# A fused two-block layer stack on one core: 24 extra matmuls of one other form in each weight unit of the last stage

## The chip, the cores and the metric

The kernel runs on one core of a Trainium2 chip. The metric is the device time of one execution in microseconds (us), as the median over the runs shown. Engines: TensorE (PE in the profile, its weight loads PEld), VectorE (DVE), ScalarE (ACT), GpSimd (POOL), SyncE (SP, which issues most DMAs).

## What is computed

The activation has 256 tokens of 2048 features. Four layers run one after the other: two of a first kind (a pooling or a recurrent mixer, a gated output product, and a second gated product), two of a second kind. The second kind, which ends the program, is in short:

```python
def hybrid_layer(x, ...):
    h = rms_norm(x, norm_g)
    proj = h @ w_in
    ...
    y_a = mla_branch(...) * jax.nn.silu(z_a)
    y_b = sgu_branch(...) * jax.nn.silu(z_b)
    y_c = gla_branch(...) * jax.nn.silu(z_c)
    g = jax.nn.sigmoid(gate_logits...).reshape(B, S, N_BRANCH, D)
    merged = (g[:, :, 0] * (y_a @ w_branch[0])
              + g[:, :, 1] * (y_b @ w_branch[1])
              + g[:, :, 2] * (y_c @ w_branch[2]))
    return x + merged @ w_out
```

All data are fp32. The last stage of the program is `merged @ w_out` of the last layer, a 256x2048 by 2048x2048 product, and the sum with x.

## The kernel before

**Weights.** The weights of all layers lie in DRAM as one stream of 1144 units. A unit is eight tiles of 128x128 fp32 (512 KB). SyncE loads unit n into one of four slots of `raw`. ScalarE writes its copy rounded to `fp32r`, TensorE's reduced fp32, into `w_hi` (line 890), VectorE the rest raw - w_hi into `w_lo` (line 1272). The semaphores `raw_in`, `hi_done`, `lo_done` and `pe_mark` pass a unit from one engine to the next and free its slots.

**Activations.** They are kept feature by feature in partitions, a tile of 128 features at a time, with the rounded value of the 256 tokens in columns 0:256 and the rest in columns 256:512. `xs` (16 tiles) holds a stage's normed input, `inner`, `latent`, `y_abc` and `merged` the inner ones. A tile of `xs` is 512 fp32 long in a partition, so neighbouring tiles lie 2 KiB apart.

**A unit on TensorE.** In `products` (lines 515 to 548) a tile of weights is stationary and 256 columns stream. For each of the eight tiles of a unit, `w_hi` times the rounded value (line 535) and `w_hi` times the rest (line 536), 16 matmuls; then TensorE waits for `lo_done` and does `w_lo` times the rounded value (line 543), eight matmuls. The last of these frees the unit's slots.

```python
if c == 0:
    if side is not None:
        side.run(at_unit(s, i, u) - 1)
    pe.wait_ge(lo_done, unit)
```

A product of the last stage has 16 tiles deep, thus two units, and ends in a bank of PSUM that VectorE evicts (line 1713), adding x. Every tensor instruction is issued with its own weight load.

**Other streams.** Stages whose result is wanted token by token (`token_products`, lines 550 to 575) exchange the operands: 128 columns of `xs` are stationary, and 512 columns of `w_hi` (line 565) or `w_lo` (line 573) stream, eight and four of them a unit. Attention, gated linear attention and norms are plain fp32 matmuls, put between the high and the low matmuls of a unit (`side.run`) or around them: line 742 (one column), line 624 (128 columns, `keep_warm`), line 874 (256 columns), line 657 (64 columns, which `g_q` yields in blocks of 1, 2, 4 or 8 neighbours with gaps as wide as the block). Each is recorded as two matmuls.

**PSUM.** Eight banks: four in `banks`, one `ms_bank`, three in `pm`. The last stage uses `banks` alone.

**The last stage.** It is named `wo`, has four turns of four products, eight units a turn and 32 in all, and no side work. VectorE and ScalarE only split weights and evict in it. SyncE stores the results, the last four tiles one by one (line 497).

Of the kernel before, what the change touches and what calls it, by code (L numbers as in the profile page):

```python
# [21 lines left out]
P = 128  # L22
HALF = P // 2
T = 256
# [141 lines left out]
def build(nc, weights, x_in, p_in, channels, inv_counts, tables, positions, w_a2, w_s, b_s, x_scratch,  # L166
          out):
    with ExitStack() as ctx:
        def sb(name, shape, dt=F32, into=ctx):
            return into.enter_context(nc.sbuf_tensor(name, shape, dt))  # L170
# [6 lines left out]
        w_hi = sb("w_hi", [P, SLOTS, UNIT], F32R)  # L177
        w_lo = sb("w_lo", [P, SLOTS, UNIT], F32R)
        sb("xs_offset", [P, 112])
        xs = sb("xs", [P, ND, 2 * T], F32R)  # L180
# [25 lines left out]
        def place(name, at, shape, dt=F32):  # L206

            with ExitStack() as over:
                if at:
                    sb(f"under_{name}", [P, int(at * 256)], F32, over)  # L210
                return sb(name, shape, dt, over)[:]

        inner, wide = place("inner", 0, [P, NI, 2 * T], F32R), place("wide", 64, [P, NI, T])
# [5 lines left out]
        y_abc, merged = place("y_abc", 0, [P, 24, 2 * T], F32R), place("merged", 48, [P, ND, 2 * T], F32R)  # L219
# [32 lines left out]
        pm = ctx.enter_context(nc.psum_tensor("pm", [P, 3, 2 * T], F32))  # L252
# [48 lines left out]
        stages = []  # L301
# [80 lines left out]
        def at_unit(s, i, u):  # L382

            return s.unit0 + i * s.units + u - named[s.layer, "latent"].unit0
# [35 lines left out]
        def read_of(s, i, j):  # L420

            e = s.readers[j]
            return READ[e], i * s.readers.count(e) + (s.read0[e] + s.readers[:j + 1].count(e))
# [5 lines left out]
        def product_bank(s, i, j):  # L429

            b, half = s.bank(i, j), slice(T, 2 * T) if s.fed and i == 1 else slice(0, T)
            if s.by_token:
                half = slice(0, 2 * T)
            return banks[:, b, half] if b < BANKS else pm[:, b - BANKS, half]

        def occupant(s, i, j):

            n, b = stages.index(s), s.bank(i, j)
            while True:
                j -= 1  # L440
                if j < 0:
                    i, j = i - 1, s.width - 1
                if i < 0:
                    n -= 1
                    if n < 0:
                        return None
                    s = stages[n]
                    i, j = s.turns - 1, s.width - 1
                if s.bank(i, j) == b:
                    return s, i, j  # L450
# [63 lines left out]
        def _(pe):  # L514
            def products(s, i, ready, after, side):
                tile = 0
                for j, p in enumerate(s.products):
                    bank = product_bank(s, i, j)
                    held = occupant(s, i, j)
                    if held is not None:  # L520
                        pe.wait_ge(*read_of(*held))
                    k = 0
                    while k < p.depth:
                        u, c = divmod(p.first_tile + k, UNIT_TILES)
                        n = min(p.depth - k, UNIT_TILES - c)
                        slot = (s.unit0 + u) % SLOTS
                        unit = i * s.units + (s.unit0 + u + 1)
                        if c == 0:
                            pe.wait_ge(hi_done, unit)
                        for t in range(n):  # L530
                            if ready is not None:
                                ready(j, k + t)
                            w = slice((c + t) * P, (c + t + 1) * P)
                            x = p.operand(i, k + t)
                            nc.tensor.matmul(bank, w_hi[:, slot, w], x[:, 0:T], start=(k + t == 0), stop=False)  # L535
                            nc.tensor.matmul(bank, w_hi[:, slot, w], x[:, T:2 * T], start=False, stop=False)  # L536
                        if c == 0:
                            if side is not None:
                                side.run(at_unit(s, i, u) - 1)
                            pe.wait_ge(lo_done, unit)  # L540
                        for t in range(n):
                            w = slice((c + t) * P, (c + t + 1) * P)
                            ins = nc.tensor.matmul(bank, w_lo[:, slot, w], p.operand(i, k + t)[:, 0:T],  # L543
                                                   start=False, stop=(k + t == p.depth - 1))
                        ins.then_inc(pe_mark, 1)
                        k += n
                    if after is not None and j == after[0]:
                        after[1]()

            def token_products(s, i, side):  # L550

                for j in range(2):
                    held = occupant(s, i, j)
                    if held is not None:
                        pe.wait_ge(*read_of(*held))
                depth, per_unit = s.units * UNIT_TILES // 4, UNIT_TILES // 4
                for u in range(s.units):
                    slot, unit = (s.unit0 + i * s.units + u) % SLOTS, i * s.units + (s.unit0 + u + 1)
                    pe.wait_ge(hi_done, unit)
                    for r in range(per_unit):  # L560
                        k, w = u * per_unit + r, slice(r * 2 * T, (r + 1) * 2 * T)
                        x = s.products[0].operand(i, k)
                        for j in range(2):
                            for at in (j * P, T + j * P):
                                nc.tensor.matmul(product_bank(s, i, j), x[:, at:at + P], w_hi[:, slot, w],  # L565
                                                 start=(k == 0 and at < T), stop=False)
                    side.run(at_unit(s, i, u) - 1)
                    pe.wait_ge(lo_done, unit)
                    for r in range(per_unit):
                        k, w = u * per_unit + r, slice(r * 2 * T, (r + 1) * 2 * T)  # L570
                        x = s.products[0].operand(i, k)
                        for j in range(2):
                            ins = nc.tensor.matmul(product_bank(s, i, j), x[:, j * P:(j + 1) * P],  # L573
                                                   w_lo[:, slot, w], start=False, stop=(k == depth - 1))
                    ins.then_inc(pe_mark, 1)
# [249 lines left out]
            for n, s in enumerate(stages):  # L825
# [7 lines left out]
                elif s.name in ("squared", "wo"):  # L833
                    def ready(j, k, b=stages[n - 1].base["p"]):
                        if j == 0:
                            pe.wait_ge(pool_done, b + k + 1)
# [20 lines left out]
                for i in range(2 if s.fed else 1 if s.by_rows else 0, s.turns):  # L857
                    if s.by_token:
                        token_products(s, i, side)
                        continue  # L860
                    if s.name == "pooled":
                        pe.wait_ge(tile_split, i * 8 + 8)
                    elif s.name == "lru":
                        pe.wait_ge(pool_done, stages[n - 1].base["p"] + i * 8 + 8)
                    products(s, i, None if i else ready, after, side)
# [1385 lines left out]
```

## Time and profile before

| what | us |
|---|---|
| median of two runs | 3346.53 |
| the two runs | 3344.90 and 3348.15 |
| span of the profiled execution, first to last instruction | 3361.6 |
| TensorE busy in it | 3322.8 (99%) |
| VectorE busy | 2291.6 (68%) |
| ScalarE busy | 1670.6 (50%) |
| GpSimd busy | 905.0 (27%) |

The page gives of the profiled execution only its span, which is longer than both timed runs. A row of a group of instructions tells its line, engine, operation, what it writes and reads, its shape and how often it stands there, then busy time and the mean duration of one. A matmul's duration holds its way through the array, in which the next one already runs, so durations of neighbours overlap. In a timeline the first number is the start in us from the span's start, the second the time from the first start to the last end of the instructions merged into the row, and a number in brackets the engine's idle time ahead of it.

### The profile page before, as it was taken

The numbers are of one execution on the slowest core, as the hardware profiler recorded it, in microseconds if no ns is written. First come the engines' busy times: TensorE is split into PE (matmuls) and PEld (weight loads), VectorE is DVE, ScalarE is ACT, GpSimd is POOL, SyncE is SP. The second block draws the span as 40 slices with busy tenths as digits, with TensorE's granted clock in tenths as the row PEclk, the third lists the DMA queues.
The fourth block names the chain that finished last, engine by engine and source line by source line (L and its number), as shares of the span: only waits on it lengthen the run. The fifth ranks groups of instructions, "written<-read, shape, count | busy, mean of one in ns | idle before, by whom it ended". The sixth has DMA issues, their size and how long they took to land.

```text
span 3361.6 us, 65406 instructions
## 1 busy us (share of the span) xinstructions
PE 3322.8 (99%) x27748; PEld 3275.0 (97%) x27748; DVE 2291.6 (68%) x2982; ACT 1670.6 (50%) x2108; POOL 905.0 (27%) x839
## 2 busy tenths in 40 slices
PE   8999999999999999999999999999999999999999
PEld 8999999999999999999899999999999999999999
DVE  7876654588878854777877755555668787655554
ACT  5334444555578844655554544444455544444443
POOL 4952320053556610332423210000004232100000
PEclk9999999999999999999999999999999999999999
DMA  6555565555655575545454455555654544555655
GB/s 233 185 186 186 187 214 188 176 185 184 198 182 181 182 237 196 176 162 181 150 172 153 156 194 195 195 194 194 195 180 166 171 152 151 190 194 193 195 191 180
DMA packets 170050, 620.20 MB, mean 184 GB/s; under 512 B 18976, under 2 KB 20640, under 8 KB 169376
## 3 DMA queue, kind: packets, MB, share of 16 engines
q1 hardware_dynamic: 165888, 602.23, 54.1%
q10 hardware_dynamic: 3872, 13.80, 1.1%
q8 instruction: 219, 3.59, 0.4%
q14 instruction: 71, 0.58, 0.1%
HBM read 610.71 MB, written 4.19 MB: 183 GB/s over the span
## 4 chain that ended last, share of the span: by engine, by line
PE 85%; DVE 6%; ACT 4%; POOL 3%; issue 1%; DMA 0%; ACTq 0%; POOLq 0%; DVEq 0%; SPq 0%
PE banks L543 20%; PE banks L535 20%; PE banks L536 20%; PE banks L565 4%; PE pm L543 3%; PE pm L536 3%; PE pm L535 3%; DVE w_lo L1272 2%; POOL win L2005 2%; PE banks L573 2%; ACT w_hi L890 2%; PE banks L607 2%; PE banks L600 2%; PE banks L602 1%; PE pm L607 1%
## 5 line engine op out<-in xcount | busy, mean ns | idle before, releaser
L1272 DVE TENSOR_TENSOR w_lo<-raw,w_hi 128x1024 fp32r<-128x1024 f32 x1144 | 1475.5, 1294 | 878.7 <-ACT w_hi L890 863.7
L890 ACT ACTIVATE w_hi<-raw 128x1024 fp32r<-128x1024 f32 x1144 | 1204.7, 1057 | 1013.0 <-PE banks L543 645.8
L535 PE MATMUL banks<-xs,w_hi 128*128 128x256 f32 x4008 | 950.0, 279 | 0.3 <-ACT val L1156 0.2
L536 PE MATMUL banks<-xs,w_hi 128*128 128x256 f32 x4008 | 949.8, 279 | 0.0
L535 PEld LDWEIGHTS banks<-xs,w_hi 128*128 128x128 f32 x4008 | 757.8, 189 | 0.9 <-ACT val L1156 0.7
L536 PEld LDWEIGHTS banks<-xs,w_hi 128*128 128x128 f32 x4008 | 757.6, 189 | 0.2
L543 PE MATMUL banks<-xs,w_lo 128*128 128x256 f32 x4008 | 553.0, 280 | 1.2 <-DVE w_lo L1272 1.2
L543 PEld LDWEIGHTS banks<-xs,w_lo 128*128 128x128 f32 x4008 | 500.6, 189 | 2.0 <-DVE w_lo L1272 1.6
L1929 POOL CAST merged<-act 128x256 fp32r<-128x256 f32 x32 | 41.1, 1285 | 714.7 <-DVE act L1709 714.7
L535 PE MATMUL pm<-xs,w_hi 128*128 128x256 f32 x952 | 223.4, 277 | 0.0
L536 PE MATMUL pm<-xs,w_hi 128*128 128x256 f32 x952 | 223.1, 277 | 0.0
L535 PE MATMUL banks<-inner,w_hi 128*128 128x256 f32 x896 | 215.5, 279 | 0.0
L536 PE MATMUL banks<-inner,w_hi 128*128 128x256 f32 x896 | 215.3, 279 | 0.0
L535 PEld LDWEIGHTS pm<-xs,w_hi 128*128 128x128 f32 x952 | 178.9, 188 | 0.1
L536 PEld LDWEIGHTS pm<-xs,w_hi 128*128 128x128 f32 x952 | 178.9, 188 | 0.1
L535 PE MATMUL banks<-y_abc,w_hi 128*128 128x256 f32 x768 | 178.8, 276 | 0.0
L536 PE MATMUL banks<-y_abc,w_hi 128*128 128x256 f32 x768 | 178.8, 276 | 0.0
L536 PEld LDWEIGHTS banks<-inner,w_hi 128*128 128x128 f32 x896 | 169.1, 189 | 0.0
L535 PEld LDWEIGHTS banks<-inner,w_hi 128*128 128x128 f32 x896 | 169.0, 189 | 0.0
L535 PEld LDWEIGHTS banks<-y_abc,w_hi 128*128 128x128 f32 x768 | 144.2, 188 | 0.0
L536 PEld LDWEIGHTS banks<-y_abc,w_hi 128*128 128x128 f32 x768 | 144.1, 188 | 0.0
L1929 POOL CAST inner<-act 128x256 fp32r<-128x256 f32 x64 | 72.6, 1134 | 259.2 <-DVE act L1754 178.2
(335 smaller groups left out, 5956.8 us busy)
## 6 DMA issues: line engine op xcount, KB each, us to landing
raw<-weights SPq DMA_DIRECT2D x1144, 512.0 KB, 3.4
wide<-x_in ACTq DMA_DIRECT2D x4, 512.0 KB, 8.7
wide<-x_in ACTq DMA_DIRECT2D x1, 2048.0 KB, 11.7
x_scratch<-wide ACTq DMA_DIRECT2D x1, 2048.0 KB, 8.5
wide<-x_scratch ACTq DMA_DIRECT2D x1, 2048.0 KB, 10.9
out_x<-wide SPq DMA_DIRECT2D x3, 512.0 KB, 6.3
w_st<-w_s ACTq DMA_DIRECT2D x2, 512.0 KB, 4.4
b_st<-b_s ACTq DMA_DIRECT2D x2, 512.0 KB, 5.3
```

The costliest lines, as they stand in the source:

```text
L535: nc.tensor.matmul(bank, w_hi[:, slot, w], x[:, 0:T], start=(k + t == 0), stop=False)
L536: nc.tensor.matmul(bank, w_hi[:, slot, w], x[:, T:2 * T], start=False, stop=False)
L543: ins = nc.tensor.matmul(bank, w_lo[:, slot, w], p.operand(i, k + t)[:, 0:T], start=False, stop=(k + t == p.depth - 1))
L565: nc.tensor.matmul(product_bank(s, i, j), x[:, at:at + P], w_hi[:, slot, w], start=(k == 0 and at < T), stop=False)
L573: ins = nc.tensor.matmul(product_bank(s, i, j), x[:, j * P:(j + 1) * P], w_lo[:, slot, w], start=False, stop=(k == depth - 1))
L600: nc.tensor.matmul(bank, w_hi[:, slot, w], operand[:, k, 0:T], start=(k == 0 and j < 4), stop=False, skip_group_check=True)
L602: nc.tensor.matmul(bank, w_hi[:, slot, w], operand[:, k, T:2 * T], start=False, stop=False, skip_group_check=True)
L607: ins = nc.tensor.matmul(bank, w_lo[:, slot, w], operand[:, k, 0:T], start=False, stop=(k == s.products[0].depth - 1), skip_group_check=True)
L890: nc.scalar.activation(w_hi[:, slot, :], raw[:, slot, :], ACT.Copy).then_inc(hi_done, 1)
L1272: nc.vector.tensor_tensor(w_lo[:, slot, :], raw[:, slot, :], w_hi[:, slot, :].bitcast(F32), ALU.subtract).then_inc(lo_done, 1)
L1929: link(nc.gpsimd.tensor_copy(dest[:, 0:T], source))
L2005: link(nc.gpsimd.tensor_tensor(dst[:, PAD:], src[:, PAD:], src[:, back:back + T], ALU.add))
```

## The change

The function `products` calls a new one, `other_shapes`, once in each unit of the last stage, ahead of the wait for `lo_done`. It issues 24 matmuls into the three banks of `pm`, every one with `start` and `stop`, so nothing is summed, and nothing reads them. The form depends on the unit (n from 0 to 31): which columns of `xs` stream (start, order, number), which tile of `w_hi` is stationary, and for the last two units the operands are exchanged.

By width, the 32 units are: 256 columns in 17 (ten starts; four other orders; one with a fixed stationary tile; two with stationary tiles that begin 16 or 64 columns further), 512 columns in ten (four starts; three other orders; a fixed stationary tile; two exchanged), and one each of 192, 224, 128, 384 and 320 columns. Together that is 10,720 columns times 24. Four of the orders read two neighbours at a time: `[[0, P], [1, 2]]` and `[[0, T], [1, 2]]` the same two again and again, `[[2, 64], [512, 2], [1, 2]]` and `[[2, P], [512, 2], [1, 2]]` two of one tile and two of the next in turn.

```diff
--- before.py
+++ after.py
@@ -537,6 +537,8 @@
                         if c == 0:
                             if side is not None:
                                 side.run(at_unit(s, i, u) - 1)
+                            if s is stages[-1]:
+                                other_shapes(i * s.units + u, slot)
                             pe.wait_ge(lo_done, unit)
                         for t in range(n):
                             w = slice((c + t) * P, (c + t + 1) * P)
@@ -546,6 +548,42 @@
                         k += n
                     if after is not None and j == after[0]:
                         after[1]()
+
+            def other_shapes(n, slot):
+
+                def moving(source, at, dims):
+                    return bass.AP(tensor=source.tensor, offset=source.offset + at, ap=[list(source.ap[0])] + [list(d) for d in dims])
+
+                x, m, h = xs[:, 0, :], merged[:, 0, :], w_hi[:, slot, :]
+                line = lambda n_: [[1, n_]]
+                tile = lambda c, at=0: moving(h, at + (c % 7) * P, line(P))
+                wide = lambda b: pm[:, b % 3, :]
+                part = lambda n_: (lambda b: pm[:, b % 3, 0:n_])
+                row = lambda c, at=0: c % 4 * 512 + at
+                shapes = (
+                    [(part(T), tile, lambda c, a=a: moving(x, row(c, a), line(T)))
+                     for a in (0, 16, 32, 48, 64, 80, 96, 112, 8, 4)]
+                    + [(part(T), tile, lambda c: moving(x, row(c, P), [[-P, 2], [1, P]])),
+                       (part(T), tile, lambda c: moving(x, row(c), [[0, P], [1, 2]])),
+                       (part(T), tile, lambda c: moving(x, row(c), [[2, 64], [512, 2], [1, 2]])),
+                       (part(T), tile, lambda c: moving(x, row(c), [[32, 16], [1, 16]]))]
+                    + [(part(n_), tile, lambda c, n_=n_: moving(x, row(c), line(n_))) for n_ in (192, 224, 128)]
+                    + [(wide, tile, lambda c, a=a: moving(x, row(c, a), line(512))) for a in (0, 32, 64, 96)]
+                    + [(wide, tile, lambda c: moving(x, row(c), [[0, T], [1, 2]])),
+                       (wide, tile, lambda c: moving(x, row(c), [[512, 2], [1, T]])),
+                       (wide, tile, lambda c: moving(x, row(c), [[2, P], [512, 2], [1, 2]]))]
+                    + [(part(n_), tile, lambda c, n_=n_: moving(x, row(c), line(n_))) for n_ in (384, 320)]
+                    + [(part(T), lambda c: tile(0), lambda c: moving(x, row(c), line(T))),
+                       (wide, lambda c: tile(0), lambda c: moving(x, row(c), line(512))),
+                       (part(T), lambda c: tile(c, 16), lambda c: moving(x, row(c), line(T))),
+                       (part(T), lambda c: tile(c, 64), lambda c: moving(x, row(c), line(T))),
+                       (wide, lambda c: moving(x, c % 7 * P, line(P)), lambda c: moving(h, 16 + c % 2 * T, line(512))),
+                       (wide, lambda c: moving(x, c % 7 * P, line(P)), lambda c: moving(h, 64 + c % 2 * T, line(512)))]
+                )
+                if n < len(shapes):
+                    to, stationary, streamed = shapes[n]
+                    for c in range(24):
+                        nc.tensor.matmul(to(c), stationary(c), streamed(c), start=True, stop=True, skip_group_check=True)
 
             def token_products(s, i, side):
 
```

TensorE's instructions in two units of the last stage (`x24` or `x8` is that many alike in a row), before:

```order
L535 MATMUL banks<-merged,w_hi 128x256
L536 MATMUL banks<-merged,w_hi 128x256
L535 MATMUL banks<-merged,w_hi 128x256
L536 MATMUL banks<-merged,w_hi 128x256
L543 MATMUL banks<-merged,w_lo 128x256 x8
L535 MATMUL banks<-merged,w_hi 128x256
L536 MATMUL banks<-merged,w_hi 128x256
L535 MATMUL banks<-merged,w_hi 128x256
L536 MATMUL banks<-merged,w_hi 128x256
```

and in the changed kernel at the same place:

```order
L535 MATMUL banks<-merged,w_hi 128x256
L536 MATMUL banks<-merged,w_hi 128x256
L535 MATMUL banks<-merged,w_hi 128x256
L536 MATMUL banks<-merged,w_hi 128x256
L586 MATMUL pm<-xs,w_hi 128x256 x24
L545 MATMUL banks<-merged,w_lo 128x256 x8
L535 MATMUL banks<-merged,w_hi 128x256
L536 MATMUL banks<-merged,w_hi 128x256
L535 MATMUL banks<-merged,w_hi 128x256
```

Between the last high-weight matmul and the eight low-weight ones, whose line is now 545, stands a row of 24 on line 586.

Further on in TensorE's stream, around the narrow forms and the first wide one, units 14 to 17 of the stage, the rows of line 586 of the changed kernel, and ahead of each the last of the stage's own high-weight matmuls:

```order
L536 MATMUL banks<-merged,w_hi 128x256
L586 MATMUL pm<-xs,w_hi 128x192 x24
L545 MATMUL banks<-merged,w_lo 128x256 x8
L536 MATMUL banks<-merged,w_hi 128x256
L586 MATMUL pm<-xs,w_hi 128x224 x24
L545 MATMUL banks<-merged,w_lo 128x256 x8
L536 MATMUL banks<-merged,w_hi 128x256
L586 MATMUL pm<-xs,w_hi 128x128 x24
L545 MATMUL banks<-merged,w_lo 128x256 x8
L536 MATMUL banks<-merged,w_hi 128x256
L586 MATMUL pm<-xs,w_hi 128x512 x24
L545 MATMUL banks<-merged,w_lo 128x256 x8
```

Here the width of the burst goes from 192 to 224, 128 and 512 columns; the stage's own matmuls stay as they were.

## Rows read from the trace of the kernel before

**Rows 1.** The page's first part: busy us (share of the span) xinstructions.

```profile
PE 3322.8 (99%) x27748; PEld 3275.0 (97%) x27748; DVE 2291.6 (68%) x2982; ACT 1670.6 (50%) x2108; POOL 905.0 (27%) x839
```

**Rows 2.** Who waited for whom, 3273 us to the end: us in total, times, longest.

```profile
ACT w_hi L890 <- PE banks L543: 47.4, 29, 1.7
DVE w_lo L1272 <- ACT w_hi L890: 29.6, 27, 1.5
...
DVE wide L1713 <- PE banks L543: 12.8, 16, 5.0
```

**Rows 3.** TensorE in the last stage: stretch, us, busy (records), granted clock, DMA share, GB/s.

```profile
3273.40:3358.60 85.20, 85.20 (x754) 1.00 0.56 184
```

**Rows 4.** Line 543 in the last stage: duration ns, first and last start.

```profile
L543 PE MATMUL banks<-merged,w_lo x256: 276/276/276, 3273.5 to 3358.6; 128*128 128x256 f32 x128
```

**Rows 5.** TensorE's timeline in the first unit of the last stage: start, us.

```profile
3273.27 0.28 PE L535 MATMUL banks<-merged,w_hi 128*128 128x256 f32 x1
3273.39 0.28 PE L536 MATMUL banks<-merged,w_hi 128*128 128x256 f32 x1
3273.50 1.07 PE L543 MATMUL banks<-merged,w_lo 128*128 128x256 f32 x8
3274.41 0.28 PE L535 MATMUL banks<-merged,w_hi 128*128 128x256 f32 x1
```

**Rows 6.** The timeline of all engines at the end of the span.

```profile
3357.82 1.07 PE L543 MATMUL banks<-merged,w_lo 128*128 128x256 f32 x8
3358.92 0.42 DVE L1713 SCALAR_TENSOR_TENSOR wide<-banks,wide 128x256 f32<-128x256 f32 x1 [5.01 <-PE banks L543]
3359.38 0.33 SPq L497 DMA_DIRECT2D out_x<-wide  x1
```

**Rows 7.** TensorE's timeline in a stage that streams 512 columns.

```profile
2487.78 1.99 PE L565 MATMUL banks<-w_hi,xs 128*128 128x512 f32 x8
2489.61 1.08 PE L573 MATMUL banks<-w_lo,xs 128*128 128x512 f32 x4
2490.53 1.99 PE L565 MATMUL banks<-w_hi,xs 128*128 128x512 f32 x8
```

**Rows 8.** TensorE's timeline: plain fp32 matmuls of 1, 128 and 256 columns.

```profile
1759.95 1.03 PE L742 MATMUL pm<-power,q_sq 128*128 128x1 f32 x8
1760.84 1.19 PE L543 MATMUL banks<-xs,w_lo 128*128 128x256 f32 x8
...
1454.77 1.61 PE L624 MATMUL pm<-mean_d 128*128 128x128 f32 x13
...
1450.90 1.03 PE L874 MATMUL ms_bank<-val,mean_d 128*128 128x256 f32 x4
1451.76 1.50 PE L624 MATMUL pm<-mean_d 128*128 128x128 f32 x12
```

**Rows 9.** TensorE in two long stretches, columns as in group 3.

```profile
1990.00:2090.00 100.00, 100.00 (x885) 1.00 0.58 192
400.00:500.00 100.00, 100.00 (x851) 1.00 0.61 209
```

**Rows 10.** TensorE's timeline around a burst of 64-column matmuls.

```profile
1575.74 0.28 PE L536 MATMUL banks<-xs,w_hi 128*128 128x256 f32 x1
...
1576.08 1.89 PE L657 MATMUL pm<-g_q,g_d 128*128 128x64 f32 x16
1577.79 1.19 PE L543 MATMUL banks<-xs,w_lo 128*128 128x256 f32 x8
1578.81 0.28 PE L535 MATMUL banks<-xs,w_hi 128*128 128x256 f32 x1
...
1579.40 0.28 PE L536 MATMUL banks<-xs,w_hi 128*128 128x256 f32 x1
```

## The prediction

> **What bounds the kernel now.** I read the page's first part, then only the last stage, because the change touches nothing else. [rows 1] shows TensorE busy for 99% of the span, VectorE for 68% and ScalarE for half. An average hides stages with other limits, so the next view is the list of waits from 3273 us to the end, which is the last stage but for its first unit [rows 2]. ScalarE waits for TensorE (47.4 us in 29 waits) to free a weight slot, VectorE waits for ScalarE (29.6 us) and, to evict a product, for TensorE (12.8 us). TensorE waits for nobody; it doesn't appear on the left of any row. The lines of the low-weight matmul say the same with a ruler: the first of them starts at 3273.5 and the last at 3358.6, granted clock 1.00, which is the 2.4 GHz level [rows 3, 4]. From the first to the last lie 31 units of 24 matmuls and seven more, 751 starts, so 85.1 / 751 = 113.3 ns from one start to the next. The rows one by one step by 0.11 or 0.12 us, across the passage from the high-weight to the low-weight matmuls too [rows 5]. The 276 ns that a row calls a matmul's duration is a pipelined one: what an added matmul costs is the start-to-start time, not 276 ns. A unit of the last stage therefore takes 24 x 113.3 ns = 2.72 us, all of it TensorE, and 32 units take 87 us.
>
> After the last matmul come one eviction by VectorE and the store of its tile [rows 6]. The change leaves that tail alone.
>
> **The change part by part.** It removes nothing and adds no wait and no DMA. Each of the 32 units gets one burst of 24 matmuls between its 16 high-weight matmuls and the wait for the low weights. The order shows it: x24 on line 586, then the eight of line 545. They write `pm` banks that nobody reads in this stage, they read `xs` and the present slot of `w_hi`, both complete. So nothing waits for them by a semaphore, but TensorE runs in order: everything behind the burst starts later by what the burst takes. Since TensorE has no idle time in the stage, no part is hidden. What moves besides is slack of others: w_hi's slots come free later, ScalarE, VectorE and the weight transfers wait longer, and all three already wait for TensorE.
>
> Now the price of a burst, by form.
>
> - 256 columns, 17 bursts (ten offsets, four orders of the same 256 elements, one fixed stationary tile, two shifted stationary tiles): 408 matmuls at the 113.3 ns of this stage, 46.2 us.
> - 512 columns, ten bursts (four offsets, three orders, a fixed tile, two with the operands exchanged): 240 matmuls. The value-by-token stages stream 512 columns: 12 starts from 2487.78 to 2490.53 us, 229 ns each [rows 7]. 240 x 229 = 55.0 us. By twice 113.3 ns it would be 54.4 us, so this hardly matters.
> - 384 and 320 columns, one burst each: 113.3 / 256 = 0.4426 ns a column, 24 x 704 x 0.4426 = 7.5 us.
> - 192, 224 and 128 columns, one burst each. No rounded-fp32 matmul under 256 columns is in the trace, so I bound it. Below: by columns, 24 x 544 x 0.4426 = 5.8 us. The nearest rows are plain fp32 ones, which carry two records per matmul, each with its weight load: eight records of one column take 0.90 us up to the next line (112 ns each), and 13 of 128 columns show the same pace (1.61 us less one drain of 0.275 us, over 12 steps: 111 ns) [rows 8]. One column costs as much as 128, so what is seen there is a floor per record of about 112 ns, and I read it as the weight load, which each added matmul has as well. 72 x 112 = 8.1 us is the value I take. Above: if narrow matmuls ran at plain fp32's pace, whose 256-column records start 0.86 / 4 = 215 ns apart [rows 8], two records to a matmul, 1.68 ns a column, 544 x 24 x 1.68 = 21.9 us.
>
> The sum is 46.2 + 55.0 + 7.5 + 8.1 = 116.8 us.
>
> One more term is a pace. The same 256-column matmul goes at two steady paces at clock 1.00: 885 of them in 100 us in one stretch (113.0 ns), 851 in another (117.5 ns), TensorE busy throughout in both [rows 9]. The slow pace appears right behind work of another form: ahead of a burst of 64-column matmuls three steps take 0.34 us, 113 ns each (1575.74 to 1576.08), and behind it five take 0.59 us, 118 ns each (1578.81 to 1579.40) [rows 10]. The change puts 32 such bursts into a stage that ran at the fast pace from end to end. Base and added matmuls together are worth 768 + 24 x 10720 / 256 = 1773 matmuls of 256 columns. All at the slow pace would cost 1773 x 4.5 ns = 8.0 us more. Most bursts have 256 or 512 columns, the rhythm of the stage itself; I take a quarter, 2.0 us, and keep 0 and 8.0 as ends. The passages between forms I take at nothing: in [rows 8] the line behind the one-column burst starts one step behind it.
>
> 116.8 + 2.0 = 118.8 us is added to the traced execution, whose span of 3361.6 us becomes 3480 us; the page tells only the span, and nothing of what lies around it. That span is 15 us above the median of the two timed runs, 3346.5 us. The last stage is a small part of either and runs at the full clock, so I add the same time to the median: 3465 us, 3.5% more.
>
> **Two rules weighed.** The trace gives 113.3 ns for 256 columns and 229 ns for 512 [rows 4, 7]. The Trainium skill ("TensorE: Matmul & The Clock Gate", section "Back-to-back issue gap") says that in a sustained stream with weight loads a matmul of 512 columns takes about 131 ns and one of 128 about 81 ns. By that figure the ten wide bursts would cost 240 x 131 ns = 31.4 us, an estimate from that page, and the sum would fall by 24 us. The trace doesn't agree with it for fp32 data, and I don't use it.
>
> Four bursts read their moving operand in pairs of neighbours (a pair repeated, or pairs taken in turn from two tiles 2 KiB apart). The trace has no such row; every one of the long stretches in [rows 4, 7] reads in one run. The Trainium skill ("Advanced Engine Details and Errata", sections "SBUF Cachelines" and "PSUM Cachelines") says that a 16-byte line wants at least two hits for full speed, which pairs of fp32 just give, and it also says that a non-contiguous pattern slows matmuls significantly. By the first the sum stands; the second is a rival below.
>
> **The rivals.**
>
> *Bursts of unusual order slow down.* For it: nothing that streams one column a cycle here does so from pairs. Against it: the 64-column matmuls of line 657 take their columns with gaps down to every second element, and still start 107 ns apart (1576.08 to 1577.79, 16 records) [rows 10], no more than the floor of 112 ns. That bounds a slowdown at some two times the contiguous pace, since 64 columns without the floor are a quarter of the 215 ns of a 256-column record, 54 ns. The four bursts cost 2 x 24 x (113.3 + 229) ns = 16.4 us at the normal pace; at half of it 16.4 us more, which makes 3482 us. The narrow ones at their upper bound add 21.9 - 8.1 = 13.8 us, alone 3479 us, both together 3495 us.
>
> *The slow pace holds for the stage.* For it: one stretch of the trace keeps it for 100 us and more without a gap [rows 9]. Against it: the end of the kernel doesn't show it. 116.8 + 8.0 = 124.8 us, so 3471 us.
>
> *The added matmuls fill a wait.* They stand ahead of the wait for the low weights. If TensorE lost time at that wait in each unit, the bursts would use it, and the time would stay near 3347 us. It decides from (118.8 - 67) / 32 = 1.6 us of idle time a unit, at which the loss falls under 2%. [rows 2, 5] show none: the first low-weight matmul starts 0.11 us behind the last high-weight one.
>
> That the change does something other than it says is excluded by the order: 32 rows of 24 stand there.
>
> **How the numbers follow.** The forecast holds with 0.62 (118.8 us added, 3461 to 3470), unusual or narrow bursts being slow 0.24 (3482), the slow pace throughout 0.12 (3471), bursts that fill idle time 0.02 (3347). The lower end is 5.8 for the narrow ones, no change of pace and 3 us of difference between runs, which the two timed runs show: 3346.5 + 114.5 - 3 = 3458. The upper end takes in half-pace pairs and the same 3 us: 3346.5 + 118.8 + 16.4 + 3 = 3485. This leaves about 1 in 10 out. A change of 2% is about what a measurement of this kernel can tell from none; 2% is 67 us, and every case but the last is well above it: slower 0.98, same 0.02, faster 0.
>
> **What would show it.** In the changed profile the last stage should be about 206 us long, TensorE without idle time in it and at clock 1.00, and everything ahead of it as before. The steps of line 586 tell each term: 0.113 us at 256 columns whatever the offset, 0.227 to 0.23 at 512, 0.112 at 128 to 224. The forecast is wrong if bursts of narrow or paired columns step clearly slower, if the matmuls of the stage itself step by 0.118, if TensorE waits for a weight slot, or if the added matmuls step by less than their columns.

## The result and the profile after

Two runs of the changed kernel took 3485.95 and 3489.11 us, median 3487.53, against 3346.53: a ratio of 1.0394, 95% interval 1.0341 to 1.0446, slower by 141.0 us. Runs more than 1.5% above the fastest of the same kernel are left out of all medians, ranges and ratios given below. The forecast was 3465 us in a range of 3458 to 3485, so the median lies 2.5 us above the range. The direction and most of the size are right. Of the 141.0 us, 22.5 are missing in the forecast, and most of them are not where I had looked.

The page of the changed kernel, first part:

```profile
span 3487.0 us, 66942 instructions
PE 3444.0 (99%) x28516; PEld 3383.6 (97%) x28516; DVE 2297.5 (66%) x2982; ACT 1670.0 (48%) x2108; POOL 899.4 (26%) x839
```

The 768 added matmuls are there (28516 - 27748), and VectorE and ScalarE have the work that they had, in a longer span [rows 1]. Who waited for whom from 3273 us to the end:

```profile
ACT w_hi L928 <- PE banks L545: 154.3, 29, 9.6
DVE wide L1751 <- PE banks L545: 86.1, 16, 16.1
DVE w_lo L1310 <- ACT w_hi L928: 81.6, 29, 7.2
```

These are the three waits of [rows 2], grown from 47.4, 12.8 and 29.6 us. TensorE still waits for nobody. From its first to its last matmul the last stage takes, before (first row) and after (second), by the same view of stretches as in [rows 3]:

```profile
3271.68:3358.61 86.93, 86.93 (x769) 1.00 0.56 181
```

```profile
3273.54:3484.10 210.56, 210.56 (x1537) 1.00 0.23 75
```

It is 123.6 us longer, without idle time and at clock 1.00. Forecast were 118.8. The timeline of TensorE gives each burst: the row of line 586, and behind it the row of line 545, whose start ends the burst. First an offset of 16, then 128 columns, then 512 contiguous columns and 512 from one pair read again and again, last the pairs taken in turn from two tiles, 256 and 512 columns:

```profile
3280.80 3.02 PE L586 MATMUL pm<-xs,w_hi 128*128 128x256 f32 x24
3283.66 1.09 PE L545 MATMUL banks<-merged,w_lo 128*128 128x256 f32 x8
...
3365.58 2.79 PE L586 MATMUL pm<-xs,w_hi 128*128 128x128 f32 x24
3368.21 1.13 PE L545 MATMUL banks<-merged,w_lo 128*128 128x256 f32 x8
...
3379.31 5.67 PE L586 MATMUL pm<-xs,w_hi 128*128 128x512 f32 x24
3384.82 1.10 PE L545 MATMUL banks<-merged,w_lo 128*128 128x256 f32 x8
...
3404.30 5.34 PE L586 MATMUL pm<-xs,w_hi 128*128 128x512 f32 x24
3409.48 0.76 PE L545 MATMUL banks<-merged,w_lo 128*128 128x256 f32 x5
...
3342.24 4.22 PE L586 MATMUL pm<-xs,w_hi 128*128 128x256 f32 x24
3346.29 0.99 PE L545 MATMUL banks<-merged,w_lo 128*128 128x256 f32 x7
...
3420.64 8.06 PE L586 MATMUL pm<-xs,w_hi 128*128 128x512 f32 x24
3428.53 1.08 PE L545 MATMUL banks<-merged,w_lo 128*128 128x256 f32 x8
```

Divided by 24 these are 119, 109.6, 229.6, 215.8, 169 and 329 ns. The same reading of all 32 bursts gives the terms of the sum:

| term | forecast us | in the trace us |
|---|---|---|
| 256 columns, 17 bursts | 46.2 | 49.0 |
| of these, the one of pairs in turn | 2.7 | 4.0 |
| 512 columns, ten bursts | 55.0 | 57.6 |
| of these, the one of pairs in turn | 5.5 | 7.9 |
| 384 and 320 columns | 7.5 | 7.7 |
| 192, 224 and 128 columns | 8.1 | 8.0 |
| bursts in all | 116.8 | 122.2 |
| the stage's own matmuls, slower | 2.0 (with the bursts' share) | 1.4 |
| last stage longer by | 118.8 | 123.6 |

So 4.8 us of the missing 22.5 lie in the stage: 3.7 in the two bursts of pairs in turn, 1.7 in the other bursts, and 0.6 less in the stage's own matmuls. The other 17 us don't lie in the changed code. The traced spans differ by 125.4 us and the medians by 141.0: the profile of before was 15 us longer than the median of its two timed runs, the one of after 0.5 us shorter than its median. The profiled execution of the changed kernel was timed too, at 3489.11 us, 2.1 us more than its span. With the same 2.1 us the profiled execution of before comes to 3363.7 us (an estimate), 17 us above the median of its two timed runs.

### The profile page after: what moved, and what is told of

Same layout as the page of the kernel before. It is cut to its first block, busy times and chain, and to the rows that moved or that the text cites. A ratio compares the mean times of both kernels' runs of the same rounds, so it can differ in the third digit from the quotient of the medians.

```text
span 3487.0 us, 66942 instructions
## 1 busy us (share of the span) xinstructions
PE 3444.0 (99%) x28516; PEld 3383.6 (97%) x28516; DVE 2297.5 (66%) x2982; ACT 1670.0 (48%) x2108; POOL 899.4 (26%) x839
## 4 chain that ended last, share of the span: by engine, by line
PE 83%; DVE 8%; ACT 4%; POOL 3%; issue 1%; DMA 1%; ACTq 0%; POOLq 0%; DVEq 0%; SPq 0%
PE banks L545 19%; PE banks L535 19%; PE banks L536 19%; PE banks L603 4%; PE pm L586 4%; DVE w_lo L1310 3%; PE pm L545 2%; PE pm L536 2%; PE pm L535 2%; POOL win L2043 2%; PE banks L611 2%; ACT w_hi L928 2%; PE banks L645 1%; PE banks L638 1%; PE banks L640 1%
## 5 line engine op out<-in xcount | busy, mean ns | idle before, releaser
L545 PE MATMUL banks<-inner,w_lo 128*128 128x256 f32 x896 | 131.8, 281 | 9.4 <-DVE w_lo L1310 9.4
```

## The experiments

The diffs are against the changed kernel unless the text says otherwise, and `...` stands for lines left out. The fast pace is 113.3 ns and the slow pace 117.8 ns from one of the kernel's own 256-column matmuls to the next.

### The same two kernels over more rounds

The edit is none.

> The changed kernel once more, timed beside the kernel before. The two profiles differ by 125.4 us (3487.0 - 3361.6), the two medians by 141.0. Theory: the change itself costs about 124 us, the length it adds to the last stage in the traces, and the other 16 us are whole executions that differ because one long stretch of the first layer (219 to 645 us) runs at the slow pace of 117.8 ns a matmul in some and at 113.3 ns in others (3600 matmuls x 4.5 ns = 16 us): then the medians here lie 124 us apart or scatter over two values 16 us apart. Rival: the change costs 141 us and the profile hides part of it; then all rounds lie 141 us apart.

The changed kernel had a median of 3490.88 us (3470.18 to 3498.94, 6 runs), the kernel before 3366.91 us (3343.90 to 3383.78, 16 runs). The ratio is 1.0362, interval 1.0324 to 1.0401, and the medians lie 124.0 us apart, what the traces say of the stage. The rival of 141 us falls: it lies above the whole interval, 109 to 135 us. The runs of the kernel before spread over 40 us. The two runs shown of before, 3344.90 and 3348.15, were at the fast end of that spread. Of the 36 later runs of the kernel before that are counted here and further down, only two were as fast. Chance seldom gives such a pair; the record doesn't tell which chip those two ran on, and whether anything set them apart stays open.

Where the spread is, or part of it, shows in a stretch of the first layer. TensorE between 240 and 600 us in the profile of before:

```profile
240.00:600.00 360.00, 360.00 (x3059) 1.00 0.58 194
```

in the first profile of the changed kernel:

```profile
240.00:600.00 360.00, 360.00 (x3059) 1.00 0.55 193
```

and in its second one, of the very same code:

```profile
240.00:600.00 360.00, 360.00 (x3179) 1.00 0.58 200
```

Busy throughout and at clock 1.00 all three times, but 117.7 ns a matmul in the first two and 113.2 ns in the third. The 3600 matmuls from the 1801st on took 424.4 us in the first two profiles and 408.5 us in the third: 16 us, decided anew in each execution. That is the size the theory gave. The last stage is not what varies: it took 210.56 us in both traces of the changed kernel, each burst the same to 0.001 us.

The rounds scatter over many values and not over two, so this stretch is one source among several. The other traces show a second one. Between 1990 and 2090 us the kernel before had 885 matmuls [rows 9]; the run with one extra matmul a unit (further down), whose code is the same up to the last stage, had 851 there, the slow pace, though its first stretch had the fast one:

```profile
1990.00:2090.00 100.00, 100.00 (x851) 1.00 0.54 187
```

Nine traces have the same code up to the last stage, the two of before and after among them. They reached it after 3254.4 to 3285.2 us. I counted the kernel's own matmuls that stand eight in a row and step by 117 to 120 ns on the mean: 2808 to 8944 of them, which cost 12 to 40 us over the fast pace. Without that cost the times to the last stage are 3238 to 3249 us, so the pace accounts for most of the spread between these traces. Which stretches made each timed run long isn't known, since only the profiled executions left a trace.

### All bursts of the stage's own form

```diff
-                shapes = (...)
+                shapes = [(part(T), tile, lambda c: moving(x, row(c), line(T)))] * 32
```

> All 32 bursts have one form, 24 matmuls of 256 columns from the start of a tile, as the stage's own ones. Theory (the pace is a matter of a burst's own form and of what it leaves behind): every burst steps by 113.3 ns and takes 2.72 us, the stage's own matmuls stay at 113.3, the last stage is 86.9 + 87.0 = 173.9 us long. Rival (any interruption of the stage's sequence can throw it into the slow pace): some bursts and some of the stage's own units step by 117.8 ns, the stage takes 176 to 181 us.

All 32 bursts and all own units ran at 113.3 ns, and the stage took 173.97 us. One of the bursts in the timeline:

```profile
3403.17 2.88 PE L567 MATMUL pm<-xs,w_hi 128*128 128x256 f32 x24
3405.89 1.07 PE L545 MATMUL banks<-merged,w_lo 128*128 128x256 f32 x8
3408.61 0.62 PE L567 MATMUL pm<-xs,w_hi 128*128 128x256 f32 x4
```

2.72 us for the burst, 2.72 us up to the next. The rival falls: an interruption as such does nothing, it is the form. The kernel took 3444.21 us, a ratio of 1.0232 (1.0197 to 1.0268), which is 66 to 90 us; 77 us by the medians, where the traces of the stage say 87, within what the spread of runs leaves open.

### Which orders of reading are slow

```diff
+ run = lambda r: (wide, tile, lambda c: moving(x, row(c), [[0, 512 // r], [1, r]]))
+ far = lambda d, r=2: (wide, tile, lambda c: moving(x, row(c), [[r, 256 // r], [d, 2], [1, r]]))
+ gap = lambda step, r: (wide, tile, lambda c: moving(x, row(c), [[step, 512 // r], [1, r]]))
...
+ shapes = ([plain] + [run(r) for r in (2, 4, 8, 16, 32, 64, 128, 256)] + [plain]
+     + [far(d) for d in (16, 64, 128, 256, 512, 1024)] + [far(512, r) for r in (4, 8, 16, 32)] + [plain]
+     + [gap(s_, 2) for s_ in (4, 8, 16)] + [gap(8, 4), gap(16, 8), gap(32, 16)]
+     + [few(n_) for n_ in (64, 16, 2)] + [plain, few(T)])
```

> The 32 bursts are other forms, most of them 512 columns wide: a run of r neighbours read again and again (r = 2 to 256), pairs taken in turn from two places 16 to 1024 elements apart, runs of 4 to 32 taken in turn from two tiles, pairs and longer runs with gaps, and contiguous ones of 64, 16 and 2 columns. Theory A (it is the length of the run: pairs are slow because each read brings only 8 bytes of use): any pattern of pairs with gaps steps like the alternating pairs did, about 329 ns at 512 columns, and runs of 4 are at about 230 again, whatever the distance. Theory B (it is the jump between the two places): only the patterns in turn are slow, by distance, and pairs with gaps are not. On the repeated runs, which stepped by 216 ns against 229 to 236: if re-reading a line saves the difference, it is kept up to r = 16 or so and lost beyond; if the saving belongs to the stride of zero, it is kept at all r. The narrow ones step by 109 to 112 ns down to 2 columns if the weight load is the floor; if not, they fall with the columns.

TensorE's timeline: a run of 8 and one of 16 read again and again, pairs in turn from places 256 elements apart, runs of 4 in turn from two tiles, pairs with a step of 4, runs of 4 with a step of 8.

```profile
3280.56 5.34 PE L578 MATMUL pm<-xs,w_hi 128*128 128x512 f32 x24
3285.74 1.08 PE L545 MATMUL banks<-merged,w_lo 128*128 128x256 f32 x8
3288.47 5.88 PE L578 MATMUL pm<-xs,w_hi 128*128 128x512 f32 x24
3294.19 0.51 PE L545 MATMUL banks<-merged,w_lo 128*128 128x256 f32 x3
...
3370.57 8.06 PE L578 MATMUL pm<-xs,w_hi 128*128 128x512 f32 x24
3378.46 0.97 PE L545 MATMUL banks<-merged,w_lo 128*128 128x256 f32 x7
...
3402.43 6.21 PE L578 MATMUL pm<-xs,w_hi 128*128 128x512 f32 x24
3408.48 0.74 PE L545 MATMUL banks<-merged,w_lo 128*128 128x256 f32 x5
...
3445.01 11.04 PE L578 MATMUL pm<-xs,w_hi 128*128 128x512 f32 x24
3455.88 0.88 PE L545 MATMUL banks<-merged,w_lo 128*128 128x256 f32 x6
...
3485.55 5.76 PE L578 MATMUL pm<-xs,w_hi 128*128 128x512 f32 x24
3491.15 0.52 PE L545 MATMUL banks<-merged,w_lo 128*128 128x256 f32 x3
```

| 512 columns as | ns a matmul |
|---|---|
| one run | 233 |
| 2, 4 or 8 elements again and again | 216 |
| 16 / 32 / 64 and more again and again | 238 / 237 / 233 |
| pairs in turn, 16 to 1024 elements apart | 328 to 329 |
| runs of 4 / 8 / 16 / 32 in turn from two tiles | 252 / 243 / 240 / 236 |
| pairs with a step of 4 / 8 / 16 | 453 / 461 / 431 |
| runs of 4, 8 and 16 with gaps as long | 233 / 233 / 237 |

Theory B falls: the distance makes no difference, and pairs with gaps are slow without any turn. Theory A has a main part of the cause, the length of the run, but not all of it, and its number for gaps was too low: 453 ns, about twice a contiguous read, not 329. Pairs in turn and pairs with gaps have runs of the same length. They differ in what lies around a pair: the ones in turn read all of 256 neighbouring elements at each of two places, the others leave out what lies between the pairs. Runs of four neighbours are free of the slowdown when they have gaps, and cost 252 ns when they alternate; why alternating costs them anything isn't shown. The saving of a repeated run holds up to 8 elements, 32 bytes, and is gone at 16, a little earlier than expected. The bursts of 64 and 16 columns took 108 ns a matmul. The one of 2 columns took 122 ns, and the own matmuls behind it 213 ns at the lower clock, which the expectation didn't foresee; the narrow bursts further down take this up.

The Trainium skill ("Advanced Engine Details and Errata", section "SBUF Cachelines") speaks of 16-byte lines and of at least two hits on each for full speed. The lines of 16 bytes fit these rows: 233 ns with four fp32 of a line in use. The two hits don't: with two of each line in use, at steps of 4, 8 and 16, the pace is about halved. The measurement decides: a stream of fp32 that went on to a new line each time needed the line whole. A pair read again and again, which uses half of one line, didn't (216 ns).

### One extra matmul a unit

```diff
+                shapes = ([one(T)] * 4 + [one(T, 16)] * 4 + [one(T, 32)] * 4 + [one(128)] * 4 + [one(192)] * 4
+                          + [one(512)] * 4 + [one(320)] * 4 + [one(2)] * 4)
...
-                    for c in range(24):
+                    for c in range(1):
```

> One extra matmul a unit in place of 24, four units in a row with each of eight forms (256 at offset 0, 16 and 32; 128; 192; 512; 320; 2 columns). Theory (what sets the pace is how the sequence resumes behind a matmul of another form): behind a 256-column one at offset 0 the own matmuls stay at 113.3 ns, behind those of other widths some units run at 117.8 ns. Rival (only a burst of a slow form brings the slow pace): all own matmuls stay at 113.3. The last stage is 86.9 + 4 x (3 x 113 + 3 x 112 + 229 + 142) ns = 91.1 us by the rival, up to 3.5 us longer by the theory.

The stage took 92.55 us, 1.5 us more than the rival's 91.1. Pace of the own matmuls behind each form, four units in a row, read from the 16 high-weight matmuls of the next unit (the eight low-weight ones right behind the extra matmul step by 113 to 130 ns):

| extra matmul | pace behind it |
|---|---|
| 256 at offset 0 | fast, four times |
| 256 at offset 16 | fast, four times |
| 256 at offset 32 | slow, fast, slow, fast |
| 128 columns | slow, fast, slow, fast |
| 192 columns | fast, four times |
| 512 columns | slow, fast, slow, fast |
| 320 columns | slow, fast, slow, fast |
| 2 columns | slow, three times, and a last unit cut short |

In the timeline of line 569, 256 columns at offset 32: behind the first of these rows the unit is fast, behind the second slow.

```profile
3312.61 0.28 PE L569 MATMUL pm<-xs,w_hi 128*128 128x256 f32 x1
3312.73 1.09 PE L545 MATMUL banks<-merged,w_lo 128*128 128x256 f32 x8
3313.66 0.28 PE L535 MATMUL banks<-merged,w_hi 128*128 128x256 f32 x1
...
3315.47 0.28 PE L569 MATMUL pm<-xs,w_hi 128*128 128x256 f32 x1
3315.59 1.10 PE L545 MATMUL banks<-merged,w_lo 128*128 128x256 f32 x8
3316.53 0.28 PE L535 MATMUL banks<-merged,w_hi 128*128 128x256 f32 x1
...
3318.41 0.28 PE L569 MATMUL pm<-xs,w_hi 128*128 128x256 f32 x1
```

From the start of line 535 to the next extra matmul lie 16 steps: 1.81 us, 113 ns each, then 1.88 us, 118 ns each. One matmul in 25 is enough, and within this run the outcome repeats: the rival falls. The time of the whole kernel, 3366.61 us, is at 1.0009 (0.9978 to 1.0039) of before; the 5.6 us by which the stage is longer drown in the spread of the runs.

### What leads back to the fast pace

```diff
+ kick = one(T, 32)
+ for form in (one(T), one(T, 16), ..., one(192), one(224), ...):
+     shapes += [kick, form]
...
+                    for c in range(1):
```

> One extra matmul a unit: in the even units a 256-column one at offset 32, which in the run before turned the pace of the own matmuls over (fast to slow, slow to fast), in the odd ones one of another form (256 at offset 0, 16, 8, 4, 48, 64, 112; 192, 224, 160, 384, 448 columns; a run of 8 and of 2 read again and again; a shifted stationary tile). Theory (the slow pace is one of two ways in which the sequence can lock, and what lies between decides which): some forms lead to the fast pace from the slow one, among them 256 at offset 16 and 192 columns, behind which four units of four were fast; 256 at offset 0 leaves the pace as it finds it. Rival (the pace after a form doesn't depend on the form): fast and slow come without relation to it.

From the slow pace, 256 columns at offset 4, 48 and 112, 192, 384 and 448 columns, and a pair read again and again led to the fast one. Offsets 0, 8, 16 and 64, 160 and 224 columns, a run of 8, and the shifted tile left it slow. So half of my guess holds (192 columns), and the other half falls (offset 16 keeps what it finds: fast in the run before, slow here). The form at offset 32 made every fast unit slow, eight times, but turned a slow one fast only once in eight; in the run before it had done so both times. So the form and the pace that it meets don't settle the outcome between them; what else does, no run here shows. The rival falls all the same: offset 32 turned the fast pace into the slow one eight times of eight here, while in the run before offsets 0 and 16 and 192 columns kept it twelve times of twelve. That 192 columns lead out of the slow pace rests on a single unit here, since in the run before all four met the fast one. Behind 192 columns:

```profile
3330.92 0.25 PE L574 MATMUL pm<-xs,w_hi 128*128 128x192 f32 x1
3331.01 1.11 PE L545 MATMUL banks<-merged,w_lo 128*128 128x256 f32 x8
3331.96 0.28 PE L535 MATMUL banks<-merged,w_hi 128*128 128x256 f32 x1
...
3333.77 0.28 PE L574 MATMUL pm<-xs,w_hi 128*128 128x256 f32 x1
```

16 steps in 1.81 us, the fast pace.

### One matmul of 192 columns in every eighth unit

```diff
                             pe.wait_ge(lo_done, unit)
+                            if s.name in ('pooled', 'silu', 'squared', 'lru', 'mix', 'wo') and u % 8 == 0:
+                                nc.tensor.matmul(ms_bank[:, T:T + 192], w_hi[:, slot, 0:P], xs[:, 0, 0:192],
+                                                 start=True, stop=True, skip_group_check=True)
```

The line stands ahead of the wait. The base is the kernel before, not the changed one.

> The kernel before with one extra matmul of 192 columns in every eighth unit of the stages pooled, silu, squared, lru, mix and wo, into an unused half of the norm's bank. Behind 192 columns the own matmuls ran at the fast pace, from either pace, in five units of five. Theory (the slow pace is a lock that a 192-column matmul opens): the long slow stretches go, the 1800 matmuls of a stretch take 204 us and not 212, the median falls below that of the kernel before by 10 to 20 us in those executions that had slow stretches, less some 80 x 0.12 = 10 us for the extra matmuls themselves; the scatter of the rounds narrows. Rival (the pace of a long stretch is set by something else than what lies ahead of it): no change but the extra 10 us, and the same scatter.

> The same with 256 columns in place of 192, a form that left the pace as it found it. Both theories: the slow stretches stay as in the kernel before, and the time is that of the kernel before plus 80 x 0.113 = 9 us, up to the scatter of the rounds. Against the run with 192 columns it tells the effect of the form from that of the extra work.

With 192 columns the median was 3351.92 us (3343.61 to 3360.68, 12 runs), with 256 columns 3369.62 us (3349.60 to 3393.37, 12 runs), the kernel before 3368.06 us (3340.74 to 3385.66, 20 runs). The ratios are 0.9954 (0.9930 to 0.9978) and 1.0012 (0.9979 to 1.0046). With 192 the spread shrinks from 45 to 17 us and the median falls by 16 us (7 to 24 by the interval), although 86 matmuls are added; with 256 neither happens. A gain of 0.5% is below the 2% at which a change counts as faster here, but its interval leaves 1 out.

The two traces show it at one place. From 220 us on both kernels are at the slow pace; at 240 us comes the first extra matmul that meets it. The two stretches ahead of it and well behind it, with 192 columns first, then with 256:

```profile
220.00:240.00 20.00, 20.00 (x171) 1.00 0.74 246
262.00:600.00 338.00, 338.00 (x2985) 1.00 0.61 200
```

```profile
220.00:240.00 20.00, 20.00 (x171) 1.00 0.76 251
262.00:600.00 338.00, 338.00 (x2872) 1.00 0.59 193
```

Both start with 171 matmuls in 20 us. Then one has 113.2 ns a matmul, the other 117.7. Over the whole traces, by the pace ahead of each of the 86 extra matmuls and of the high-weight ones behind it: with 192 columns five met the slow pace and four of them left the fast one; with 256 columns 22 met the slow pace and none left it. At one place in each trace, at 1041 and 1048 us, the fast pace ahead was followed by the slow one, so neither form keeps the slow pace from setting in. The rival falls. The kernel isn't faster than the fastest runs of the kernel before: it takes away the long executions.

### Narrow bursts

```diff
+                few = lambda n_: (part(n_), tile, lambda c: moving(x, row(c), line(n_)))
+                shapes = [few(n_) for n_ in (128, 64, 16, 2) for _ in range(8)]
```

> The last stage's bursts are narrow: eight units each with bursts of 128, 64, 16 and 2 columns. Theory (an added matmul costs its weight load, about 112 ns, whatever its columns, at clock 1.00): 32 x 24 x 0.110 = 84 us more than before. Rival (bursts with few columns lower the granted clock): the 16- and 2-column units, or those behind them, show a clock of 0.5 and own matmuls at 213 ns, and the stage is longer by 20 us or more beyond that.

By stretches, one for each width from 128 down to 2:

```profile
3262.00:3305.50 43.50, 43.50 (x388) 1.00 0.33 108
3305.50:3349.00 43.50, 43.50 (x387) 1.00 0.33 110
3349.00:3400.00 51.00, 51.00 (x370) 0.81 0.30 93
3400.00:3457.00 57.00, 56.81 (x380) 0.74 0.08 26
```

The bursts themselves cost what the theory says wherever the clock held, 109.5 ns a matmul at 128 columns and 108.2 at 64, 16 and 2; others of 16 and 2 columns took up to 124.5 ns. But from the second burst of 16 columns on the granted clock fell to its lower level, 1.2 GHz, again and again (mean 0.81 and 0.74), without a pause of TensorE ahead of it, and at that level the own matmuls stepped by 213 ns. The stage took 196.45 us; 86.9 + 84 would be 171. Both had a part of it right: the floor is real, and so is the clock. That the floor is the weight load is my reading of it; no run here leaves a weight load out or makes it narrower. The forecast had three narrow bursts of 128 columns and more; their rows show clock 1.00.

### The changed kernel without pairs in turn

```diff
-                       (part(T), tile, lambda c: moving(x, row(c), [[2, 64], [512, 2], [1, 2]])),
+                       (part(T), tile, lambda c: moving(x, row(c), line(T))),
...
-                       (wide, tile, lambda c: moving(x, row(c), [[2, P], [512, 2], [1, 2]]))]
+                       (wide, tile, lambda c: moving(x, row(c), line(512)))]
```

> The changed kernel with its two bursts of pairs taken in turn from two tiles made contiguous, 256 and 512 columns. Theory (these two cost 4.04 and 7.89 us in place of some 2.8 and 5.6, and nothing else hangs on them): the last stage is 210.6 - 1.2 - 2.3 = 207.1 us from its first to its last matmul. Rival (they also change the pace of what follows): it differs from that by a microsecond or more.

```profile
3264.18:3471.31 207.13, 207.13 (x1537) 1.00 0.23 76
```

207.13 us, 3.4 us less than the changed kernel: as worked out, to 0.03 us. The rival falls, though the unit behind the first of the two bursts did change its pace, from 114.7 to 117.8 ns a matmul, worth 0.07 us.

## Why the prediction was right or wrong

**What bounds the stage.** Right. TensorE waited for nothing, the bursts lengthened the others' waits and nothing hid them. The rival of bursts that fill a wait is out.

**256 and 512 columns.** The mechanism was right. Without the two bursts of pairs in turn, those of 256 columns took 45.0 us (forecast 43.5) and those of 512 columns 49.7 us (forecast 49.5). The burst of offset 0 took 113.3 ns as forecast, eleven of the 17 took 117.8 to 119.6, and those of 512 columns 229 to 233.5 (forecast 229) but for the pairs. The step that failed is "0.113 us at 256 columns whatever the offset": the form has a price of its own in this stream that I had put at nothing. The burst at offset 16 stepped by 119.2 ns on the mean, though it began from the fast pace.

**Narrow bursts.** Right: 8.0 us against 8.1. The floor read from plain fp32 rows of one and 128 columns [rows 8] carried over, 109.5 to 111.5 ns against 112. The upper bound of 21.9 us was far off.

**Pairs.** The forecast priced all four bursts of pairs like contiguous ones, and for the two in turn this step failed: 11.9 us in place of 8.2. A rival had that part, but "at half of it 16.4 us more" was too much and for all four. Pairs in turn cost 1.4 times the contiguous pace, 3.4 us against contiguous bursts in the same place; pairs read again and again cost less than a contiguous run (216 against 233 ns). The prediction also weighed that a non-contiguous pattern slows matmuls; in the Trainium skill ("Advanced Engine Details and Errata", section "PSUM Cachelines") this stands under PSUM. Every burst wrote its PSUM bank in one run, so these runs don't test it. The bound of some two times, drawn from the gapped columns of [rows 10], held for every order tried: 461 ns against 233 at most.

**The pace.** The reading that two paces exist at clock 1.00 [rows 9, 10] and that work of another form can bring the slow one is shown. The term was 2.0 us; the own matmuls lost 1.4 us, and the bursts, beside the two of pairs in turn, took 1.7 us more than forecast. What I missed is the consequence for the base. I took the slow stretch of [rows 9] for a property of the kernel before. It is a property of an execution.

**The base.** This is the step that failed by most: "3 us of difference between runs, which the two timed runs show", and with it the addition to 3346.5 us. Two runs that agree within 3 us say little when 16 more spread from 3344 to 3384. The span of the profile, 15 us above both, was a warning in plain sight, and I passed it over with "the last stage is a small part of either". Against the median of those 16 runs, the changed kernel's 3490.88 us is 124.0 us more, 5.2 from the forecast's 118.8; the interval of that ratio, 1.0324 to 1.0401, is 109 to 135 us. That the base was low is shown; why these two runs were that fast is not.

## What to carry to other kernels

Price an added matmul by the start-to-start time of its neighbours and, below 256 columns, by a floor of some 108 to 112 ns a matmul with its own weight load. When a profile's span and the timed median differ by more than the timed runs among themselves, find out by more rounds what an execution can do before adding a small term to one of them. And count matmuls over long busy stretches: 3059 against 3179 in the same 360 us is a loss that no list of waits shows.

## What the runs showed of the hardware that I had not expected

- A stream of 256-column fp32r matmuls, each with its weight load, has two steady paces at full clock, 113.3 and 117.8 ns. One matmul in 25 of another form can change which, and the choice can last for hundreds of microseconds. Some forms did the same in every case seen in the last stage (256 columns at offset 0 kept the pace), one didn't (offset 32). Why a form decides, and what decides beside it, isn't settled.
- One such matmul of 192 columns every eighth unit took 16 us off the median (7 to 24), and four of the five that met the slow pace ended it; of 22 matmuls of 256 columns that met it, none did.
- The moving operand's order matters by runs of 16 bytes: pairs of fp32 with gaps 431 to 461 ns for 512 columns, runs of four with gaps 233, and 216 when no more than 32 bytes are read again and again, 17 ns less than a contiguous read of 512 columns.
- A single 2-column matmul took 27 ns up to the next one, but the 24 matmuls behind it took 2.91 us in place of 2.72 or 2.83. Together that is 0.11 us more than a slow unit, the price of one matmul of the narrow bursts (108 ns), so the 27 ns are not what it costs.
